# VectorE's order in a delta iteration: 32x128 value transpositions, sums of squares as fp32r passes, gate copy ahead of a chunk

## The reference, cut to what matters

```python
def l2norm(t):
    tf = t.astype(jnp.float32)
    return tf * lax.rsqrt(jnp.sum(tf * tf, -1, keepdims=True) + NORM_EPS)

def gated_deltanet(h, w_in, conv_w, a_log, dt_bias, norm_w, w_out):
    proj = h @ w_in
    qkv, z, b, a = jnp.split(proj, ...)
    qkv = jax.nn.silu(causal_depthwise_conv(qkv, conv_w))
    q, k, v = jnp.split(qkv, [GDN_DQK, 2 * GDN_DQK], axis=-1)
    q = jnp.repeat(l2norm(q...) * HEAD_DIM ** -0.5, rep, axis=2)
    k = jnp.repeat(l2norm(k...), rep, axis=2)
    ...
    o = gated_delta_rule(q, k, v, g, beta)
    o = o * lax.rsqrt(jnp.mean(o * o, -1, keepdims=True) + NORM_EPS)
    o = (o.astype(h.dtype) * norm_w) * jax.nn.silu(z...)
    return o.reshape(B, S, GDN_DV) @ w_out
```

## Time and profile before

| | us |
|---|---|
| median of three runs | 2680.84 |
| lowest and highest | 2679.5, 2681.04 |
| the profiled execution, whole time | 2680.55 |
| its span | 2678.9 |
| TensorE matmul busy | 2628.5 (98%) |
| VectorE busy | 1997.6 (75%) |
| ScalarE busy | 1221.8 (46%) |
| GpSimd busy | 865.7 (32%) |

### The profile page before, as it was taken

The page is one execution under the profiler, slowest core; times in us unless marked ns, Lnnn a source line. Parts: engine busy times, 40 slices in busy tenths (PEclk is TensorE's granted clock), DMA queues, the critical chain, the costliest instruction groups (busy, mean ns, idle before and its releaser), DMA issues.

```text
span 2678.9 us, 44567 instructions
## 1 busy us (share of the span) xinstructions
PE 2628.5 (98%) x16843; PEld 2205.9 (82%) x16843; DVE 1997.6 (75%) x2523; ACT 1221.8 (46%) x1604; POOL 865.7 (32%) x646
## 2 busy tenths in 40 slices
PE   6999999999999999999999999999999999999998
PEld 4798899899887888888888888899777778888887
DVE  1487887788798687777777777689999996655554
ACT  2365556545665445343343343354333334444344
POOL 1076777777767404500000000014555550000000
PEclk8999999999999999999999999999999999999999
DMA  9966776776676776666666666655555555666664
GB/s 364 361 222 216 232 244 217 233 236 220 211 250 202 229 202 221 190 193 189 189 192 191 188 190 193 189 160 174 169 170 168 173 176 180 191 189 187 190 204 153
DMA packets 283972, 552.47 MB, mean 206 GB/s; under 512 B 16881, under 2 KB 54322, under 8 KB 282674
## 3 DMA queue, kind: packets, MB, share of 16 engines
q1 hardware_dynamic: 263488, 473.49, 57.2%
q0 software_dynamic: 19472, 76.06, 8.0%
q10 hardware_dynamic: 866, 0.80, 0.1%
HBM read 548.19 MB, written 2.10 MB: 205 GB/s over the span
## 4 chain that ended last, share of the span: by engine, by line
PE 82%; DVE 14%; DMA 2%; issue 1%; SPq 1%; ACT 0%; DVEq 0%
PE pg L1201 40%; PE pd L1201 18%; PE pg L930 5%; PE pg L943 4%; PE pg L1188 4%; DVE pd L2068 3%; DVE arena L2068 2%; PE pg L962 2%; DVE arena L2142 1%; DMA wr<-in_gdn_w_in 1%; PE pd L856 1%; DVE arena L2302 1%; DVE arena L2234 1%; DVE arena L2237 1%; DVE arena L2208 1%
## 5 line engine op out<-in xcount | busy, mean ns | idle before, releaser
L1794 ACT ACTIVATE wh<-wr 128x1024 fp32r<-128x1024 f32 x616 | 652.9, 1061 | 927.0 <-PE pg L1201 581.4
L2341 DVE TENSOR_TENSOR wl<-wr,wh 128x1024 fp32r<-128x1024 f32 x615 | 771.5, 1266 | 381.4 <-ACT wh L1794 378.1
L670 POOL TENSOR_TENSOR wl<-wr,wh 128x1024 fp32r<-128x1024 f32 x195 | 485.3, 2497 | 266.3 <-ACT wh L1575 127.3
L1201 PE MATMUL pg<-wh,hh 128*128 128x512 f32 x1344 | 528.9, 394 | 0.3 <-DVE hl L2417 0.3
L1201 PE MATMUL pg<-wl,hh 128*128 128x512 f32 x1344 | 527.3, 392 | 0.0
L1201 PE MATMUL pg<-wh,hl 128*128 128x512 f32 x1344 | 525.7, 391 | 0.0
L1575 ACT ACTIVATE wh<-wr 128x1024 fp32r<-128x1024 f32 x216 | 227.8, 1057 | 324.9 <-PE pg L943 163.5
L1201 PEld LDWEIGHTS pg<-wh,hh 128*128 128x128 f32 x1344 | 252.5, 188 | 59.5 <-DVE wl L2341 2.4
L943 PE MATMUL pg<-hh,wh 128*128 128x256 f32 x1024 | 299.9, 293 | 0.8 <-ACT arena L1635 0.8
L1201 PEld LDWEIGHTS pg<-wh,hl 128*128 128x128 f32 x1344 | 252.4, 188 | 56.4
L1201 PEld LDWEIGHTS pg<-wl,hh 128*128 128x128 f32 x1344 | 252.3, 188 | 54.4
(11 more groups left out here) (451 smaller groups left out, 4873.1 us busy)
## 6 DMA issues: line engine op xcount, KB each, us to landing
wr<-in_w_in SPq DMA_DIRECT2D x224, 512.0 KB, 3.8
wr<-in_ffn_w_gu SPq DMA_DIRECT2D x176, 512.0 KB, 3.8
wr<-in_gdn_w_in SPq DMA_DIRECT2D x128, 512.0 KB, 4.4
arena<-in_mod_w POOLq DMA_DIRECT2D x60, 1024.0 KB, 6.6
wr<-in_ffn_w_down SPq DMA_DIRECT2D x88, 512.0 KB, 4.6
arena<-in_mod_w SPq DMA_DIRECT2D x32, 1024.0 KB, 13.6
wr<-in_gdn_w_in SPq DMA_DIRECT2D x128, 256.0 KB, 3.2
wr<-in_gdn_w_out SPq DMA_DIRECT2D x56, 512.0 KB, 4.7
```

Source lines behind the costliest of these rows:

```text
L670: nc.gpsimd.tensor_tensor(wl[c % RING][:], wraw[c % 4], wh[c % RING][:].bitcast(F32), ALU.subtract)\
L1201: m = nc.tensor.matmul(halves(bank)[:, h, :], act[x][:, k0 + k, h * P:(h + 1) * P], w[s][:, k, :], skip_group_check=True, start=(first and ...
L1794: a(wh[c % 4][:], wraw[c % 4], ACT.Copy).then_inc(s_hc, 1)
L2341: v.tensor_tensor(wl[c % 4][:], wraw[c % 4], wh[c % 4][:].bitcast(F32), ALU.subtract).then_inc(s_lc, 1)
```

## The change

Six things change in the delta iterations.

1. The sums of squares become four fp32r passes: the squares come as a high part and a low part. VectorE squares q and k into vtok (`squares`), ScalarE squares them again into fp32r (`squares_high`), and GpSimd subtracts (`squares_low`) in place over vtok. TensorE waits for the subtraction. `squares_high` stands between the two Silu calls; `squares_low` stands behind the low part of chunk 0 of the next group and its mod_load, ahead of the low part of chunk 1; in the opening it stands behind that of chunk 1.
2. VectorE's `squares` moves from behind "oz" to ahead of the wait for "o1".
3. ScalarE's first z_out moves from behind the conversion of a chunk to ahead of it.
4. The v transpositions become 32 of 32x128 (one chunk of tokens and all four heads each) for 16 of 32x256 (both chunks), in a new order: the first 16 in steps 4 to 13, the others in steps 14 and 16.
5. "md0" and "o0" are two steps, so there are 19 steps; the modulation halves move: half 11 from step 11 to step 12 and into SBUF, halves 12 and 13 from 14 and 15 to 15 and 16, 14 and 15 from 16 to 17.
6. In the last iteration two `o_low` move from steps 4 and 6 to steps 5 and 15.

```diff
-MOD_HALVES = {0: (0, 1), **{t: (t - 1,) for t in range(3, 11)}, 11: (10, 11), 14: (12,), 15: (13,), 16: (14, 15)}
-V_TURNS = {3: (0, 2), 4: (2, 4), 8: (4, 6), 9: (6, 8), 10: (8, 10), 12: (10, 14), 13: (14, 16)}
-LATE_LOWS = (0, 1, 2, 4, 6)
+MOD_HALVES = {0: (0, 1), **{t: (t - 1,) for t in range(3, 13)}, 15: (12,), 16: (13,), 17: (14, 15)}
+V_TURNS = {4: (0, 3), 9: (3, 6), 10: (6, 8), 11: (8, 11), 12: (11, 13), 13: (13, 16), 14: (16, 24), 16: (24, 32)}
+LATE_LOWS = (0, 1, 2, 5, 15)
...
-        sqb = Xb.rearrange("p a b -> p (a b)")
+        sq_s = [over("sqh", arena_at + 4 * xb_at, 8 * P), over("sql", arena_at + 4 * vtok_at, 8 * P)]
...
+            def squares_low(g):
+                pool.wait_ge(s_sq1, g + 1)
+                pool.wait_ge(s_sqh, g + 1)
+                nc.gpsimd.tensor_tensor(sq_s[1][:], fl(vtok), sq_s[0][:].bitcast(F32), ALU.subtract).then_inc(s_sql, 1)
...
                         if t < 2:
                             mod_load(it * 8 + 40, t)
+                        if t == 0:
+                            squares_low(it + 1)
...
             for t in range(RING):
                 low(1, t)
+                if t == 1:
+                    squares_low(0)
...
-                pe.wait_ge(s_sq1, it + 1)
+                pe.wait_ge(s_sql, it + 1)
...
                 for n in range(2):
-                    m = nc.tensor.matmul(pd[0][:, n * 512:(n + 1) * 512], ones[:], sqb[:, n * 512:(n + 1) * 512],
-                                         start=True, stop=True)
+                    for i in range(2):
+                        m = nc.tensor.matmul(pd[0][:, n * 512:(n + 1) * 512], ones_r, sq_s[i][:, n * 512:(n + 1) * 512],
+                                             start=(i == 0), stop=(i == 1))
...
+            def squares_high(g):
+                act.wait_ge(s_qk, g + 1)
+                a(sq_s[0][:], fl(qk), ACT.Square).then_inc(s_sqh, 1)
...
                 if more:
                     silu_qk(it + 1)
+                    squares_high(it + 1)
                     silu_v(it + 1)
...
                 nc.scalar.preload_act_table_set("natural_log_exp_and_others")
-                yield
                 if more:
                     z_out(it + 1, 0)
+                yield
                 V("o1")
...
             gh(1, 1)
+            squares_high(0)
             z_out(0, 0)
...
-                fq = qk.rearrange("p a b -> p (a b)")
-                v.tensor_tensor(sqb, fq, fq, ALU.mult).then_inc(s_sq1, 1)
+                v.tensor_tensor(fl(vtok), fl(qk), fl(qk), ALU.mult).then_inc(s_sq1, 1)
...
                 mod_sum(it, 0)
+                yield
                 PEw("o0")
...
-                if not mods:
+                if mods:
+                    squares(it + 1)
+                else:
                     low(0, 0, 0)
                 PEw("o1")
...
                 done(v.tensor_tensor(oz, ob, zt, ALU.mult))
-                if mods:
-                    squares(it + 1)
...
-                    i, q = slice(32 * (n // 4), 32 * (n // 4) + 32), slice(32 * (n % 4), 32 * (n % 4) + 32)
-                    v.transpose(vtok[i, :, q].rearrange("p (c h) t -> p c h t", c=TT),
-                                vT[q].rearrange("p h (c t) -> p c h t", c=TT)[:, :, :, i])
+                    c, i, k = n // 16, n // 4 % 4 * 32, n % 4 * 32
+                    m = v.transpose(vtok[i:i + 32, c * VH:c * VH + VH, k:k + 32],
+                                    vT[k:k + 32, :, c * P + i:c * P + i + 32])
+                    if n == 31:
+                        link(m)
...
-                    held = range(4, 16) if 2 <= half < 8 else range(8) if 8 <= half < 12 else range(0)
+                    held = range(4, 16) if 2 <= half < 8 else range(6) if 8 <= half < 11 else range(0)
...
-                for t in range(18):
+                for t in range(19):
...
-                    if isinstance(j, int) and t == 16:
+                    if isinstance(j, int) and t == 17:
                         o_low(0)
                         o_low(1)
```

More of the change, by code:

```diff
@@ L221, in build @@
         zt = take(8, P)
+        xb_at = at[0]
         Xb = take(8, P)
@@ L429, in build @@
         s_sq1 = sem("s_sq1")
+        s_sqh = sem("s_sqh")
+        s_sql = sem("s_sql")
         s_ot = sem("s_ot")
@@ L2366, in _ @@
                     mod_half(LATE, n // 2, n % 2, range(2, 12) if 1 <= n < 6 else range(0))
-                if t == 16:
+                if t == 17:
                     for i in range(3):
```

## The result

The changed kernel takes 2688.80 us in the median of seven runs (2688.43 to 2690.25), the one before 2679.78 (2679.07 to 2681.04): ratio 1.0033, 95% interval [1.0023, 1.0042]. The forecast was 2673.5, with a range up to 2688; the time lies above both. The profiled execution took 2690.02, its span 2688.4, 9.5 more than the span before.

The account below looks back on a forecast made before the run. TensorE was taken as the bound, busy 91.38 of 92.32 us per inner iteration. Terms -4.4 + 0.6 - 0.4 - 0.7 - 2.5 + 0.3 = -7.1 took 2680.55 to 2673.5 us; the 8-in-10 range was 2666 to 2688.

Parts of the forecast that it names:

- The port: Modulation half at 418.57 against GpSimd's pass at 418.64: VectorE gets in first, leaving a 0.1 wait; +0.6 over six iterations.
- The rival: GpSimd's pass gets in first at 418.6, holding VectorE's accumulations: +1.2 instead of +0.1 in six iterations, 2680; chance 0.24.
- What is moved lands in the idle 3.66 ... so 1.6 remain: Moved VectorE work fits idle time around L2248; L2252 ends about 420.4, TensorE wants it at 422.00, 1.6 us spare.
- VectorE's order, -0.75: In the inverse, fewer transpositions ahead of TensorE's waits remove the 0.6 and 0.15: -4.4 over six iterations.
- Sums against ScalarE, net 0: At each boundary, 0.80 saved by fp32r passes becomes new ScalarE waits of 0.5 and 0.2: net 0.
- the rival in which ScalarE has more room: The sums' 0.80 saving counts at 7 boundaries because ScalarE is not late: 2668; chance 0.14.
- Transpositions, 0.30 each: Each 32x128 transposition on VectorE takes 0.30, bounds 0.22 to 0.44; VectorE pays +2.6 per iteration.
- The slower rival: Transpositions cost the same whatever their size, 0.44 each; L2252 misses TensorE, +2.6 in each of six iterations: 2693; chance 0.14.
- Square in Silu's table: ScalarE's Square needs no table load between Silu calls; otherwise two more loads of 1.28 per boundary, 2691, chance 0.06.
- Last boundary, -0.7: Before the last iteration, shorter passes cut into the waits of 1.5 and 0.7: -0.7, between -0.8 and 0.
- Last iteration, -2.5 + 0.3: Moving an output split removes most of a 2.2 wait and 1.6 clock loss, -2.5; a half behind eight transpositions adds +0.3.
- Opening: In the opening, GpSimd's new subtraction comes just at the sums' start: -0.4, between -0.8 and 0.

Follow-up runs that it names:

- wide version: Changed kernel with 16 transpositions of 32x256 again, all in steps 4 to 13, instead of 32 of 32x128: 2674.19 us, ratio 0.9976 to the kernel before.
- the sums alone: Kernel before with only the fp32r sums of squares, earlier squares and earlier first gate copy; order and transpositions as before: 2682.03 us, ratio 1.0005.
- the order alone: Changed kernel with the fp32 sums of before, keeping VectorE's new order, 19 steps and 32x128 transpositions: 2686.67 us, ratio 1.0023 to the kernel before.
- The move alone: Kernel before with only the last iteration's two output splits by VectorE moved from steps 4 and 6 to 5 and 15: 2678.81 us, ratio 0.9993.

## Why the prediction was wrong, by its own steps

- **The port: the first step that failed.** "I take it that VectorE gets in first" had 0.07 us of margin, and I priced the contest at +0.1 per iteration. GpSimd's pass came where I had it, 1.33 behind the start of r (418.64 before, 608.35 after). VectorE came 0.39 later than my 418.57 allows (1.65 behind r, not 1.26): 0.17 because the eight transpositions took 2.57 (605.32 to the next operation at 607.89) and not 2.4, 0.10 between the start of the copy ahead of them and the first of them, and 0.11 because that copy, with no idle time ahead of it any more, started late itself. So the pass was 0.32 ahead of the accumulation. "r to v1" and "v1 to flips" cost 1.21 + 0.51 = 1.7 per iteration. The rival had this mechanism and its four held accumulations (5.2 forecast, 5.12 measured), but at 1.2 per iteration in all, which gave 2680. It had 1.4 of waits for these 1.7, and it missed what follows.
- **The second step that failed, and the larger one:** "What is moved lands in the idle 3.66 ... so 1.6 remain". It put the transpositions' 2.6 us at nothing. The period missed its forecast by 2.0 (93.70 for 91.67). With half 13 ahead of the eight transpositions 0.8 of that comes back (92.88); with wide transpositions, early, all of it does (91.64), and narrow ones at that same place cost 1.9 (93.52). I also counted VectorE's load as work. Of its 8.5 us more, 2.6 are work. In the timeline of after it waits for nobody between 557.95 and its wait at 624.17, where before it had 3.66 and 2.68 of idle time, so what holds it up anywhere in this stretch makes everything behind late. The run with half 13 first shows it: nearly the forecast course, and still 92.88. The Trainium skill ("SBUF — State Buffer", SBUF: two separate sides) describes such an exclusive lock; the 0.76 that becomes 2.78 beside a pass agrees. I drew on it for one slot and should have for all.
- **VectorE's order, -0.75: right.** The wide version's gain over the sums alone lies in "sums to r", 76.61 to 75.75, -0.86; with fp32 sums it is 77.23 to 76.35, -0.88; the order alone, with the narrow ones, has 76.41, -0.82.
- **Sums against ScalarE, net 0: right in sum, and nearly in its parts.** 0.80 was forecast as saved; from the first pass to the flips it is 1.04 against 1.72, so 0.68. The wait at the gate copy is 0.5, as forecast, but "flips to sums" grows by 0.77: in the wide version the last product before the wait starts at 611.95 and the next at 612.73, where 0.12 is normal, and that one takes 0.11 longer. So the sums alone are 0.15 slower per iteration, and the rival in which ScalarE has more room falls. The term that was mis-sized is the wait, 0.77 for 0.5. In the changed kernel this wait is 0.26, since TensorE is already late, and 0.52 appears at "on", where I had 0.2. I did not see that `squares_low`, for which GpSimd idled 2.85 until VectorE's late squares, pushes GpSimd's next pass into "on".
- **Transpositions, 0.30 each: right** (301 ns mean, 9.6 for 32). The slower rival (same cost whatever the size) falls.
- **Square in Silu's table: right.** There is one table load per boundary, as before:

```profile
614.96 1.07 ACT L1655 ACTIVATE arena<-arena 128x1024 f32<-128x1024 f32 x1
616.07 1.06 ACT L1660 ACTIVATE sqh<-arena 128x1024 fp32r<-128x1024 f32 x1
617.03 1.04 ACT L1665 ACTIVATE arena<-arena 128x1024 f32<-128x1024 f32 x1
618.09 1.28 ACT L1744 ACT_TABLE_LOAD   x1
```

- **Last boundary, -0.7: wrong, +3.2.** Waits of 0.9 at v1, 0.9 for ScalarE's second gate copy, 0.5 for the modulation sum and 1.5 at "on": the inner iteration's lateness, with a split of the output in front of everything. In the wide version this stretch is 93.99 against 94.06, so the -0.7 itself does not come either.
- **Last iteration, -2.5 + 0.3: right**, -2.7 (the move alone -2.8). The clock loss went with the stall. Before, the granted clock was 0.68 over 840 to 845, which is 31 us behind the row product, after 5 us in which TensorE was busy for 2.79. The same place in after is 851.87, and the clock is 1.00 there as in every 5 us from 820.90 to 905.90:

```profile
851.87:856.87 5.00, 5.00 (x81) 3.70 (x80) 2.63 (x4) 2.48 (x4) 3.11 (x3) 1.00 0.34 115
```

- **The sum.** Opening -0.1 for -0.4, six iterations +8.7 for -3.8, boundary +3.2 for -0.7, last iteration -2.7 for -2.2, behind it +0.3 for 0: +9.4 (9.5 before rounding) for -7.1. The forecast of 2673.5 is close to the wide version (2674.19), in part by luck: against before, that one has +0.1 in the opening, -4.2 in six iterations, -0.1 at the boundary, -2.8 in the last iteration and +0.5 behind it. Two slips in my sums change little: six times 0.75 is 4.5 and not 4.4, and the single terms in the slower rival are -3.3 and not -3.7. Not settled is how the changed kernel's 2.1 us per iteration divide. VectorE is busy for 84.7 there and for 79.5 in the wide version: 2.6 of these 5.2 are the transpositions' own work and the rest is time in which it is held. No run took GpSimd's passes away while it kept the rest.

## What to carry to other kernels

An engine that is busy for 75% of the program can still be the bound in a stretch: VectorE was busy for 76.2 of an iteration's 92.35 us, and 2.6 us more of work on it cost TensorE 1.9 to 2.1. Count from its last real idle gap to the deadline; where no gap is left, added work counts nearly whole, and each pass of the other engine that holds it comes on top. Where two engines race for a shared port with a margin below a tenth of a microsecond, put both outcomes into the sum. A matmul made cheaper is worth what its helpers leave: here 0.68 saved on TensorE met one Square on ScalarE and one subtraction on GpSimd and was gone.

## What was unexpected in the hardware

- GpSimd gets in between two of VectorE's operations that stand back to back: the second starts up to 2.0 late (0.76 becomes 2.78). VectorE's transpositions, with one input, ran beside a pass nearly at their own length: eight in 2.53 from 605.31, with half 13 first, while GpSimd's pass ran from 605.57 to 607.97.
- Accumulations with one input in SBUF and one in PSUM were not held: 0.75 each in the mean, 17 before and 15 after, where those with both inputs in SBUF took 1.06 and 1.31.
- A wait of TensorE costs more than it shows: 0.50 in the view of waits was 0.77 between starts, 1.05 was 1.21, 0.26 was 0.52. In each, 0.16 is the view's: it counts from the end of the last matmul's record, and the records overlap (0.28 long at 0.12 apart, 0.39 at 0.23). The first product behind the two shorter waits also took 0.11 longer than its record's usual 0.28.
